# Half a 64-byte line between the weight tiles and the activation tiles of a two-block float32 transformer on one core

## The chip, the cores and the metric

One core of a Trainium2 chip runs the whole program in one launch. The metric is device time in microseconds (us), the median of several executions. Before the change it is 1710.91 us, the median of three runs between 1709.13 and 1711.71.

## The reference, cut to what matters

Two transformer blocks of different kinds, each two layers deep, work on x of 256 tokens by 1024 features in float32. Nearly all of the arithmetic is products of activations with weight matrices that come from HBM:

```python
for l in range(2):                                   # first block
    h = rms_norm(x, attn_norm[l]) @ w_in[l]          # then three kinds of attention
    x = x + mix @ w_o[l]
    gate, up = split(rms_norm(x, ffn_norm[l]) @ w_gate_up[l])
    x = x + (silu(gate) * up) @ w_down[l]            # 2816 hidden features
for l in range(2):                                   # second block
    h = rmsnorm(x, ...) @ w_in_2[l]                  # pool, convolution, dilated attention, gates
    x = x + rmsnorm(merged @ w_out_2[l], ...)
    x = x + rmsnorm(memory_cross_attention(...), ...)
    x = x + rmsnorm((silu(conv(h @ up_a)) * (h @ up_b)) @ w_down_2[l], ...)
```

## The kernel before, in words

**Layout.** Everything is feature-major: a tile `[128, k, 256]` holds 128 features of a slot k in its partitions and the 256 tokens along the free axis, 1024 bytes a slot. T is 256, PAIR is 512 and KD, the number of slots of x, is 8.

**Products.** Each float32 operand is split in a high part, rounded to the format fp32r, and a low part, the rest. A product is then three matmuls: low weights by high activations (L775, in `products`), high weights by low activations (L777), high by high (L778). `first_products` does the same for the first jobs after a norm (L732, L735, L741). There the stationary operand, read by a weight load (LDWEIGHTS), is a 128x128 piece of a weight tile, and the moving operand is a 256-column slot of an activation tile. Jobs with `feature=False` turn the roles round (L784, L786, L787): activations are loaded, weights move.

**Weights.** They are packed by the host in chunks of 1536 columns, 6144 bytes in each partition. SyncE issues the DMAs (L2540) into a ring of five tiles `raw`; ScalarE rounds a chunk into one of four `weights_hi` (L636, `split_hi`); VectorE writes raw minus high into one of four `weights_lo` (L647, `split_lo`), GpSimd for a few chunks (L660, `pool_lo`). A chunk's slots come free when TensorE is past them. Jobs are in a fixed order for each layer, written out by hand; each engine follows it with its own helpers.

**SBUF.** `place` puts tiles one behind the other, each rounded up to 8 words (32 bytes). The 13 weight tiles come first, then `x`, `y`, `squares`, then `minus_half`, and behind that `x_hi` and `x_lo`, the norm's small tiles, `row`, `quiet`, the gains, the constants (with the identity matrix `ident` for transposes) and the area `arena`, in which both blocks keep their mixing and feed-forward activations at different times:

```python
def place(name, cols, dt=F32, at=None):
    ...
    at = cursor[0]
    cursor[0] += -(-n // 8) * 8
...
X = place("x", (KD, T))
Y = place("y", (KD, T))
SQ = place("squares", (KD, T))
HALF = place("minus_half", 16)
XH = place("x_hi", (KD, T), F32R)
XL = place("x_lo", (KD, T), F32R)
```

`HALF` is filled with -0.5 once (L2626) and read as an exponent by six small GpSimd operations (L1401). `QUIET` is filled with zeros (L2625); `keep_busy` (L708) multiplies it with itself, one column broadcast to 128, in front of some waits of TensorE.

Of the kernel before, what the change touches and what calls it, by code (L numbers as in the profile page):

```python
# [298 lines left out]
def gain_places(block):  # L299
    at, n = {}, 0  # L300
    for name, c in gain_columns(block):
        at[name] = n
        n += 1 if c == -1 else abs(c)
    return at, n
# [103 lines left out]
def transformer(nc, known, stream_a, jobs_a, stream_b, jobs_b, const_at,  # L408
                x_in, mem_in, pos_in, w_a, w_b, gains_a, gains_b, consts, out):
    ctx = ExitStack()  # L410
    with ctx:
# [10 lines left out]
        def place(name, cols, dt=F32, at=None):  # L422

            cols = (cols,) if isinstance(cols, int) else cols
            n = math.prod(cols)
            if at is None:
                at = cursor[0]
                cursor[0] += -(-n // 8) * 8
            assert at + n <= end, (name, at + n, end)
            t = nc.alloc_sbuf_tensor_at(name, [P, *cols], dt, offset=base + 4 * at)  # L430
            return t
# [22 lines left out]
        X = place("x", (KD, T))  # L454
        Y = place("y", (KD, T))
        SQ = place("squares", (KD, T))
        HALF = place("minus_half", 16)
        XH = place("x_hi", (KD, T), F32R)
        XL = place("x_lo", (KD, T), F32R)
        PART = place("merge_part", PAIR)  # L460
# [7 lines left out]
        OROOT = place("dif_root", 16)  # L468
        OFACT = place("dif_factor", 16)
        T1 = place("t1", PAIR)  # L470
        T2 = place("t2", PAIR)
        ROW = place("row", 64)
        QUIET = place("quiet", 8)
        _, na = gain_places(0)
        _, nb = gain_places(1)
        GA = place("gains_a", (DEPTH, na))
# [228 lines left out]
        def keep_busy(ps, n):  # L705

            for _ in range(n):
                nc.tensor.matmul(ps[:, T:T + P], QUIET[:, 0:1].to_broadcast([P, P]), QUIET[:, 0:1].to_broadcast([P, P]), start=True, stop=True, skip_group_check=True)  # L708

# [689 lines left out]
        def pool_power(dst, src, half):  # L1399

            return nc.gpsimd.tensor_tensor(dst, src, half, ALU.pow)  # L1401

        def pool_factor(pl, pool, l, name):
# [3 lines left out]
            pool.wait_ge(*s.at(l, "qk_mean", QK_NAMES[b - 1]))  # L1407
            pool_power(HFACT[:, a:b, 0:4], HROOT[:, a:b, 0:4], HALF[:, 0:12].rearrange("p (a n) -> p a n", n=4)).then_inc(*s.mark("by_pool", name))

# [10 lines left out]
        def pool_dif_factor(pl, pool, l):  # L1420

            s = A
            pool.wait_ge(*s.at(l, "dif_root"))
            pool_power(OFACT[:, :], OROOT[:, :], HALF[:, :]).then_inc(*s.mark("by_pool", "dif"))

        def tensor_a(pe, l):
            A.layer = l
# [1166 lines left out]
        def pool_layer(pl, pool, l, order):  # L2594
            pl.s.layer, pl.s.writing = l, "pool"
            pl.pool_next, pl.pool_ahead = pl.pool_ahead, 0
            for kind, name in order:
                if kind == "first_chunks":
                    pool_lo(pl, pool, l, 1)
                if kind == "mem_squares" and l == 0:  # L2600
                    pool_mem_sum(pool)
                if kind == "adds" or kind == "norm":
                    pool_norm(pl, pool, l, name)
                elif kind == "roots" and name in ("uk", "uq"):
                    pool_factor(pl, pool, l, name)
                elif kind == "scale" and name[0] == "u":
                    pool_scale(pl, pool, l, name)
                elif kind == "dif_sum":
                    pool_dif_factor(pl, pool, l)
                elif kind == "job":  # L2610
                    pool_lo(pl, pool, l, pl.last_chunk(name) + 2)
                    if name == "down3":
                        pool_next_chunks(pl, pool, l)
# [10 lines left out]
        def _(dve):  # L2624
            nc.vector.memset(QUIET[:, :], 0.0)  # L2625
            nc.vector.memset(HALF[:, :], -0.5)  # L2626
            nc.vector.memset(eps_col, EPS).then_inc(*O.mark("eps"))
# [70 lines left out]
```

## Time and profile before

| | us |
|---|---|
| median of three runs | 1710.91 |
| the profiled execution, as timed | 1712.45 |
| its span, from the first to the last instruction | 1710.6 |
| TensorE matmul busy | 1672.5 |
| TensorE weight load busy | 1610.7 |
| VectorE busy | 1195.9 |
| ScalarE busy | 895.9 |
| GpSimd busy | 113.9 |

TensorE's mean granted clock is 0.996 of full speed. Matmuls are pipelined, so that the duration of one (some 280 ns) is longer than the time from the start of one to the start of the next (some 115 ns). The latter is what adds up to the span; it is had by dividing a stretch that has no break by the matmuls in it. Each stretch counts an instruction that crosses its edge, so a count can be two or three too high.

### The profile page before, as it was taken

How to read it: one execution, taken by the hardware profiler on the slowest of the kernel's cores; microseconds unless marked ns; L12 is line 12 of the kernel's file. 1: busy time of each engine (PE TensorE's matmuls, PEld its weight loads, DVE VectorE, ACT ScalarE, POOL GpSimd, SP SyncE). 2: the span in 40 equal slices, each digit the busy share in tenths (PEclk: the TensorE clock that was granted, in tenths of full speed). 3: DMA queues.
4: the chain of work that ended last, by engine and by line, in shares of the span. 5: the costliest groups of instructions: out<-in, count | busy, mean ns of one | idle time of the engine just before them, and what ended most of it. 6: DMA issues, size and time to landing. Idle time of an engine off the chain costs nothing.

```text
span 1710.6 us, 31850 instructions
## 1 busy us (share of the span) xinstructions
PE 1672.5 (98%) x13590; PEld 1610.7 (94%) x13590; DVE 1195.9 (70%) x1745; ACT 895.9 (52%) x1366; POOL 113.9 (7%) x72
## 2 busy tenths in 40 slices
PE   9989999999899999999999999999999999999997
PEld 9978999999789999989999989999899999899997
DVE  5887767557867675476758768973667768669863
ACT  5575544455765444544545765544534446656542
POOL 2020000020100000210000110001100001010000
PEclk9999999999999999999999999999999999999999
DMA  8313555554235555545345335555445445346550
GB/s 290 101 63 122 193 187 178 174 194 139 75 108 194 197 180 182 214 163 189 112 137 192 122 131 202 199 171 176 157 154 168 140 148 185 117 148 202 198 184 28
DMA packets 52830, 274.31 MB, mean 160 GB/s; under 512 B 6096, under 2 KB 6736, under 8 KB 52560
## 3 DMA queue, kind: packets, MB, share of 16 engines
q1 hardware_dynamic: 52544, 271.22, 46.6%
q8 instruction: 107, 1.75, 0.4%
q10 hardware_dynamic: 144, 1.05, 0.2%
q14 instruction: 35, 0.29, 0.0%
HBM read 271.19 MB, written 1.05 MB: 159 GB/s over the span
## 4 chain that ended last, share of the span: by engine, by line
PE 81%; DVE 13%; ACT 3%; issue 2%; DMA 1%; SPq 0%; ACTq 0%; DVEq 0%
PE bank L775 17%; PE bank L778 17%; PE bank L777 17%; PE scores L775 3%; PE scores L777 3%; PE scores L778 3%; DVE weights_lo L647 2%; PE heads L775 2%; PE heads L778 2%; PE heads L777 2%; DVE x_lo L900 1%; PE scores L1849 1%; ACT probs L1170 1%; PE heads L1877 1%; DVE x L2340 1%
## 5 line engine op out<-in xcount | busy, mean ns | idle before, releaser
L647 DVE TENSOR_TENSOR weights_lo<-raw,weights_hi 128x1536 fp32r<-128x1536 f32 (+2 forms) x344 | 584.2, 1715 | 244.3 <-ACT weights_hi L636 243.9
L636 ACT ACTIVATE weights_hi<-raw 128x1536 fp32r<-128x1536 f32 (+4 forms) x352 | 499.8, 1439 | 210.6 <-PE bank L778 87.2
L775 PE MATMUL bank<-x_hi,weights_lo 128*128 128x256 f32 (+1 forms) x1600 | 452.4, 283 | 0.8 <-DVE weights_lo L647 0.8
L778 PE MATMUL bank<-x_hi,weights_hi 128*128 128x256 f32 (+1 forms) x1600 | 446.5, 279 | 0.0
L777 PE MATMUL bank<-x_lo,weights_hi 128*128 128x256 f32 (+1 forms) x1600 | 446.1, 279 | 0.0
L775 PEld LDWEIGHTS bank<-x_hi,weights_lo 128*128 128x128 f32 (+1 forms) x1600 | 298.2, 186 | 6.1 <-issue 4.8
L777 PEld LDWEIGHTS bank<-x_lo,weights_hi 128*128 128x128 f32 (+1 forms) x1600 | 298.8, 187 | 2.0 <-issue 2.0
L778 PEld LDWEIGHTS bank<-x_hi,weights_hi 128*128 128x128 f32 (+1 forms) x1600 | 298.5, 187 | 0.0
L775 PE MATMUL bank<-hidden_hi,weights_lo 128*128 128x256 f32 x704 | 196.2, 279 | 0.0
L777 PE MATMUL bank<-hidden_lo,weights_hi 128*128 128x256 f32 x704 | 196.1, 279 | 0.0
L778 PE MATMUL bank<-hidden_hi,weights_hi 128*128 128x256 f32 x704 | 196.1, 279 | 0.0
L778 PEld LDWEIGHTS bank<-hidden_hi,weights_hi 128*128 128x128 f32 x704 | 133.0, 189 | 0.0
L777 PEld LDWEIGHTS bank<-hidden_lo,weights_hi 128*128 128x128 f32 x704 | 132.8, 189 | 0.0
L775 PEld LDWEIGHTS bank<-hidden_hi,weights_lo 128*128 128x128 f32 x704 | 132.2, 188 | 0.2 <-DVE hidden_lo L2194 0.2
L775 PE MATMUL scores<-x_hi,weights_lo 128*128 128x256 f32 x416 | 116.2, 279 | 0.9 <-DVE weights_lo L647 0.9
L778 PE MATMUL scores<-x_hi,weights_hi 128*128 128x256 f32 x416 | 116.3, 280 | 0.0
L777 PE MATMUL scores<-x_lo,weights_hi 128*128 128x256 f32 x416 | 116.3, 279 | 0.0
L834 POOL TENSOR_TENSOR squares<-squares 128x512 f32<-128x512 f32 x28 | 51.5, 1838 | 841.4 <-ACT squares L2123 648.3
L775 PEld LDWEIGHTS scores<-x_hi,weights_lo 128*128 128x128 f32 x416 | 78.0, 187 | 1.2 <-issue 1.2
L777 PEld LDWEIGHTS scores<-x_lo,weights_hi 128*128 128x128 f32 x416 | 78.1, 188 | 0.0
L778 PEld LDWEIGHTS scores<-x_hi,weights_hi 128*128 128x128 f32 x416 | 78.0, 187 | 0.0
L775 PE MATMUL heads<-x_hi,weights_lo 128*128 128x256 f32 x256 | 71.8, 280 | 0.4 <-DVE weights_lo L647 0.4
(410 smaller groups left out, 3395.2 us busy)
## 6 DMA issues: line engine op xcount, KB each, us to landing
raw<-in_w_b SPq DMA_DIRECT2D x194, 768.0 KB, 4.2
raw<-in_w_a SPq DMA_DIRECT2D x120, 768.0 KB, 4.3
raw<-in_w_a SPq DMA_DIRECT2D x16, 512.0 KB, 3.6
raw<-in_w_b SPq DMA_DIRECT2D x10, 512.0 KB, 4.0
raw<-in_w_b SPq DMA_DIRECT2D x2, 752.0 KB, 4.5
raw<-in_w_a SPq DMA_DIRECT2D x2, 736.0 KB, 8.6
raw<-in_w_b SPq DMA_DIRECT2D x2, 720.0 KB, 4.7
raw<-in_w_a SPq DMA_DIRECT2D x2, 672.0 KB, 7.3
```

The costliest lines, as they stand in the source:

```text
L636: nc.scalar.activation(whi[c % SPLIT][:, 0:n], raw[c % RAW][:, 0:n], ACT.Copy).then_inc(*s.mark("weights_hi", c))
L647: nc.vector.tensor_tensor(wlo[c % SPLIT][:, 0:n], raw[c % RAW][:, 0:n], whi[c % SPLIT][:, 0:n].bitcast(F32), ALU.subtract).then_inc(*s.mar ...
L775: ins = nc.tensor.matmul(dst, wl, xh, start=start, stop=False, skip_group_check=skip)
L777: nc.tensor.matmul(dst, wh, xl, start=False, stop=False, skip_group_check=skip)
L778: ins = nc.tensor.matmul(dst, wh, xh, start=False, stop=stop, skip_group_check=skip)
L834: nc.gpsimd.tensor_tensor(sq[:, 0:2, :], sq[:, 0:2, :], sq[:, 2 * n:2 * n + 2, :], ALU.add).then_inc(*s.mark("sq_pairs", (tag, n)))
L900: nc.vector.scalar_tensor_tensor(out=XL[:, k, :], in0=X[:, k, :], scalar=gains(k), in1=XH[:, k, :].bitcast(F32), op0=ALU.mult, op1=ALU.sub ...
L1170: ins = nc.scalar.activation(PA[c][:, m, :], score_bank[c][:, m * T:(m + 1) * T], ACT.Exp, scale=f[:, m:m + 1], bias=ROW[:, r + m:r + m + ...
L1849: ins = nc.tensor.matmul(dil_scores(h, m, g), QKB[r, f // 2, m * P:(m + 1) * P], QKB[r, 6 + f // 2, 0:dil_tiles(m) * P], start=True, stop= ...
L1877: ins = nc.tensor.matmul(out_bank[rows, m * P:(m + 1) * P], VB[:, kt, f * DHD:(f + 1) * DHD], PTB[:, g * kts + kt, :], start=(n == 0), sto ...
L2340: nc.vector.tensor_tensor(x, x, y, ALU.add).then_inc(*s.mark("x_new", (tag, last)))
```

## The change

`quiet` (8 words) takes the place of `minus_half` (16 words) ahead of `x_hi`, and `minus_half`, now 24 words of which the same 16 are read at most, takes the place of `quiet` behind `row`. No instruction is added, removed or moved in time; the first `memset` of `HALF` writes 24 columns where it wrote 16.

```diff
         SQ = place("squares", (KD, T))
-        HALF = place("minus_half", 16)
+        QUIET = place("quiet", 8)
         XH = place("x_hi", (KD, T), F32R)
         XL = place("x_lo", (KD, T), F32R)
         PART = place("merge_part", PAIR)
@@
         ROW = place("row", 64)
-        QUIET = place("quiet", 8)
+        HALF = place("minus_half", 24)
         _, na = gain_places(0)
@@
-            pool_power(OFACT[:, :], OROOT[:, :], HALF[:, :]).then_inc(*s.mark("by_pool", "dif"))
+            pool_power(OFACT[:, :], OROOT[:, :], HALF[:, 0:16]).then_inc(*s.mark("by_pool", "dif"))
```

In bytes from the first weight tile, whose ring and `x`, `y`, `squares` keep their places:

| tiles | place before, mod 128 | after, mod 128 |
|---|---|---|
| `raw`, `weights_hi`, `weights_lo`, `x`, `y`, `squares` | 0 | 0 |
| `x_hi`, `x_lo`, `merge_part` and the small tiles up to `row` | 64 | 32 |
| `const` (with `ident`) | 32 | 64 |
| `const_b` | 64 | 96 |
| `arena`: mix, hidden, memory and their parts | 64 | 96 |

## Rows read from the trace of the kernel before

**Rows 1.** The page: span, and busy time of each engine.

```profile
span 1710.6 us, 31850 instructions
PE 1672.5 (98%) x13590; PEld 1610.7 (94%) x13590; DVE 1195.9 (70%) x1745; ACT 895.9 (52%) x1366; POOL 113.9 (7%) x72
```

**Rows 2.** The page: the chain that ended last, by engine.

```profile
PE 81%; DVE 13%; ACT 3%; issue 2%; DMA 1%; SPq 0%; ACTq 0%; DVEq 0%
```

**Rows 3.** Stretches without a break: hidden (four rows), gate and up (last).

```profile
core 0: us, PE busy (x) PEld busy (x) DVE busy (x) ACT busy (x) POOL busy (x), PEclk, DMA share, GB/s
305.00:355.00 50.00, 50.00 (x443) 50.00 (x442) 24.50 (x19) 21.53 (x18) 0.29 (x1) 1.00 0.49 162
650.00:700.00 50.00, 50.00 (x427) 50.00 (x426) 24.51 (x19) 19.52 (x17) 0.00 (x0) 1.00 0.46 158
1140.00:1190.00 50.00, 49.97 (x441) 49.78 (x440) 24.89 (x20) 24.26 (x26) 0.90 (x1) 1.00 0.43 145
1640.00:1690.00 50.00, 50.00 (x426) 50.00 (x426) 22.30 (x17) 22.65 (x24) 3.33 (x3) 1.00 0.37 122
210.00:260.00 50.00, 50.00 (x426) 50.00 (x426) 36.74 (x43) 22.50 (x21) 0.00 (x0) 1.00 0.56 191
```

**Rows 4.** Groups by line, 302.6 to 363 us (first block, layer 0, down).

```profile
L778 PE MATMUL bank<-hidden_hi,weights_hi 128*128 128x256 f32 x176 | 48.6, 276 | 0.0
L778 PEld LDWEIGHTS bank<-hidden_hi,weights_hi 128*128 128x128 f32 x176 | 33.0, 188 | 0.0
```

**Rows 5.** The same groups, 646.3 to 709 us (layer 1, down).

```profile
L778 PE MATMUL bank<-hidden_hi,weights_hi 128*128 128x256 f32 x176 | 49.5, 281 | 0.0
L778 PEld LDWEIGHTS bank<-hidden_hi,weights_hi 128*128 128x128 f32 x176 | 33.8, 192 | 0.0
```

**Rows 6.** Stretches with the quick spacing: four of ten, and their sum.

```profile
302.60:363.20 60.60, 59.93 (x529) 1.00 0.53 184
484.40:505.70 21.30, 21.30 (x174) 1.00 0.33 103
760.40:808.80 48.40, 48.40 (x417) 1.00 0.51 171
1138.50:1198.40 59.90, 59.87 (x528) 1.00 0.49 171
...
sum 297.10, PE 296.41; mean PE 29.64
```

**Rows 7.** The whole span of one line each: L775, L784, L732.

```profile
0.00:1711.00 1711.00, 961.85 (x3416) 1.00 0.47 160
0.00:1711.00 1711.00, 136.19 (x444) 84.52 (x444) 1.00 0.47 160
0.00:1711.00 1711.00, 50.06 (x192) 35.99 (x192) 1.00 0.47 160
```

**Rows 8.** Groups by line and shape: moving `ident` (first), moving `v_b` (second).

```profile
L1105 PE MATMUL turned<-const,probs 128*128 128x128 f32 x128 | 18.0, 278 | 3.8 <-DVE probs L1147 2.6 <-DVE probs L1153 1.1
L1877 PE MATMUL heads<-probs_tb,v_b 128*64 128x128 f32 x144 | 19.1, 278 | 0.0
```

**Rows 9.** Waits: who waited for whom, us in total, times, longest.

```profile
DVE weights_lo L647 <- ACT weights_hi L636: 243.9, 137, 7.9
ACT weights_hi L636 <- PE bank L778: 87.2, 40, 3.1
PE bank L775 <- DVE weights_lo L647: 3.6, 3, 2.8
```

**Rows 10.** The moved small tiles: instructions that touch them.

```profile
L2626 DVE MEMSET minus_half<- x1: 72/72/72, 0.8 to 0.8; 128x16 f32 x1
L2625 DVE MEMSET quiet<- x1: 65/65/65, 0.8 to 0.8; 128x8 f32 x1
L1401 POOL TENSOR_TENSOR dif_factor<-dif_root,minus_half x2: 2901/2901/2901, 125.3 to 473.3; 128x16 f32<-128x16 f32 x2
```

**Rows 11.** Groups by line and shape: reads and writes of moved tiles on VectorE.

```profile
L900 DVE SCALAR_TENSOR_TENSOR x_lo<-x,gains_b,x_hi 128x256 fp32r<-128x256 f32 x48 | 19.5, 478 | 0.0
L2194 DVE TENSOR_TENSOR hidden_lo<-t,hidden_hi 128x256 fp32r<-128x256 f32 x44 | 16.6, 420 | 7.0 <-ACT hidden_hi L2156 7.0
L647 DVE TENSOR_TENSOR weights_lo<-raw,weights_hi 128x1536 fp32r<-128x1536 f32 x314 | 548.3, 1761 | 228.3 <-ACT weights_hi L636 227.9
```

## The prediction, made before the changed kernel was run

> **What bounds the kernel now.** I read the page's busy times first: TensorE is busy 98% of the span with matmuls and 94% with weight loads, VectorE 70%, ScalarE 52% [rows 1]. The chain that ended last lies on TensorE for 81%, and for 13% on VectorE [rows 2]. So the spacing of TensorE's own matmuls sets the end. Next I took stretches without a break, where all matmuls have one shape, 256 columns against a 128x128 weight load, and divided [rows 3]. Counts include what crosses an edge, so I take two off each. The down products of the first block's layer 0 come to 441 in 50 us, 113.4 ns each; those of layer 1 to 425, 117.6 ns. The same pair comes back in the second block: 439 (113.9) and 424 (117.9). Gate and up products: 424, 117.9. [...] The code, the tiles and the places in SBUF of layers 0 and 1 are the same, and other engines do much the same work (VectorE 24.5 against 24.5 us). So there are **two steady spacings**, about 113.4 and 117.8 ns, and the stream keeps the one it has fallen into. In the slow one a matmul takes 281 ns for 276, and the weight load at L778 192 for 188 [rows 4, 5]: the load is held up as well as the matmul. That looks like two streams that both read SBUF, the weight load and the moving operand, and get in each other's way depending on how they are phased.
>
> [...]
>
> [...]
>
> [...]
## The result: 1718.57 us against 1709.97, half a per cent slower

The changed kernel takes 1718.57 us, the median of five runs (1717.72 to 1719.94). The kernel before, in five runs, takes 1709.97 (1708.69 to 1711.71). The ratio is 1.0042 with a 95% interval of 1.0031 to 1.0054. Forecast was 1676 us with 0.27 on slower.

The page of the changed kernel, with the lines that answer to [rows 1, 2]:

```profile
span 1716.5 us, 31850 instructions
PE 1679.4 (98%) x13590; PEld 1618.1 (94%) x13590; DVE 1194.9 (70%) x1745; ACT 895.9 (52%) x1366; POOL 114.0 (7%) x72
...
PE 83%; DVE 11%; ACT 3%; issue 2%; DMA 1%; SPq 0%; ACTq 0%; DVEq 0%
```

The span grew by 5.9 us, TensorE's busy time by 6.9, its weight loads' by 7.4; VectorE, ScalarE and GpSimd did not change by more than 1 us. So most of the time is in TensorE's own spacing. The stretches of [rows 3], in the changed kernel; gate and up first here, then the four down stretches:

```profile
core 0: us, PE busy (x) PEld busy (x) DVE busy (x) ACT busy (x) POOL busy (x), PEclk, DMA share, GB/s
210.00:260.00 50.00, 50.00 (x430) 50.00 (x430) 37.16 (x43) 22.54 (x22) 0.00 (x0) 1.00 0.57 192
305.00:355.00 50.00, 50.00 (x425) 50.00 (x424) 24.50 (x19) 19.96 (x17) 0.00 (x0) 1.00 0.45 153
650.00:700.00 50.00, 50.00 (x425) 50.00 (x424) 24.50 (x19) 20.56 (x17) 0.00 (x0) 1.00 0.44 146
1140.00:1190.00 50.00, 50.00 (x425) 50.00 (x424) 23.42 (x21) 22.73 (x27) 0.00 (x0) 1.00 0.42 143
1640.00:1690.00 50.00, 50.00 (x425) 50.00 (x425) 24.05 (x22) 22.72 (x27) 2.10 (x2) 1.00 0.35 122
```

The quick spacing of before is gone, and there are two new ones that go with the tile. Down products, with the moving tile at 96 mod 128, count 425 in all four stretches, 423 after the two for the edges: 118.2 ns (from the start times in ns, 118.33). Gate and up, which move x at 32, count 430: 116.8 (116.67). Neither is 113.4, neither is 117.8. One long kind of stretch keeps 117.8 though x moves there at 32 as well, the products of the second block's feed-forward in both layers (a count of 427, as in the kernel before):

```profile
1060.00:1110.00 50.00, 50.00 (x427) 50.00 (x426) 46.40 (x64) 28.60 (x33) 0.00 (x0) 1.00 0.60 200
```

So the place 32 has two spacings too, 116.7 and 117.8. Products that load x and move weights lost 4.9 ns each where they had been quick (first block, from 57 us; the first row is the kernel before, the second in its own fence the changed one):

```profile
57.00:68.00 11.00, 11.00 (x100) 11.00 (x99) 10.84 (x16) 7.05 (x22) 0.00 (x0) 1.00 0.54 174
```

```profile
57.50:68.50 11.00, 11.00 (x95) 11.00 (x95) 10.84 (x16) 6.83 (x21) 0.00 (x0) 1.00 0.55 175
```

In this stretch and its fellow in layer 1 they went at 113.4 before and at 118.3 after; other stretches of the kind were at 117.8 before. Counted over the whole trace from the start times, 256-column products that do not follow a wait (intervals of 100 to 160 ns):

| products | count | before, mean ns | after, mean ns | us |
|---|---|---|---|---|
| move x | 7049 | 117.44 | 117.03 | -2.9 |
| move hidden | 2107 | 115.57 | 118.33 | +5.8 |
| load x, move weights | 830 | 115.54 | 118.27 | +2.3 |
| move mix | 454 | 116.11 | 118.33 | +1.0 |
| move memory and its heads | 377 | 115.7 | 118.4 | +1.0 |

That is +7.2 us; pool tiles and loads of 96 columns add about 1. The span of the one traced pair took 5.9 of the 8. The medians are 8.6 us apart, and the traced execution of before, at 1712.45, was slower than all five runs of that kernel in the comparison, so how much of the 8 reaches the end is known only within some 2 us.

The prediction's points 2 to 4 in the changed kernel: VectorE's groups by line and shape, then the waits (who waited for whom, us in total, times, longest), then the instruction that writes the moved small tile:

```profile
L900 DVE SCALAR_TENSOR_TENSOR x_lo<-x,gains_b,x_hi 128x256 fp32r<-128x256 f32 x48 | 19.5, 482 | 0.0
L2194 DVE TENSOR_TENSOR hidden_lo<-t,hidden_hi 128x256 fp32r<-128x256 f32 x44 | 16.7, 421 | 7.0 <-ACT hidden_hi L2156 7.0
```

```profile
DVE weights_lo L647 <- ACT weights_hi L636: 246.3, 137, 7.9
ACT weights_hi L636 <- PE bank L778: 90.2, 41, 3.2
```

```profile
L2626 DVE MEMSET minus_half<- x1: 78/78/78, 0.8 to 0.8; 128x24 f32 x1
```

VectorE reads and writes tiles half a line off at 482 and 421 ns, against 478 and 420 in [rows 11]. The waits are those of [rows 9], 2.4 and 3.0 us longer, as they should be behind a slower TensorE.

### The profile page after: what moved, and what is told of

Read it like the earlier page. It is cut to its first block, busy times and chain, and to the rows that moved or that the text cites. A ratio compares the mean times of both kernels' runs of the same rounds, so it can differ in the third digit from the quotient of the medians.

```text
span 1716.5 us, 31850 instructions
## 1 busy us (share of the span) xinstructions
PE 1679.4 (98%) x13590; PEld 1618.1 (94%) x13590; DVE 1194.9 (70%) x1745; ACT 895.9 (52%) x1366; POOL 114.0 (7%) x72
## 4 chain that ended last, share of the span: by engine, by line
PE 83%; DVE 11%; ACT 3%; issue 2%; DMA 1%; SPq 0%; ACTq 0%; DVEq 0%
PE bank L775 17%; PE bank L778 17%; PE bank L777 17%; PE scores L775 3%; PE scores L778 3%; PE scores L777 3%; DVE weights_lo L647 2%; PE heads L775 2%; PE heads L778 2%; PE heads L777 2%; PE bank L784 1%; PE bank L787 1%; PE bank L786 1%; DVE x_lo L900 1%; ACT probs L1170 1%
## 5 line engine op out<-in xcount | busy, mean ns | idle before, releaser
L647 DVE TENSOR_TENSOR weights_lo<-raw,weights_hi 128x1536 fp32r<-128x1536 f32 (+2 forms) x344 | 584.5, 1716 | 246.7 <-ACT weights_hi L636 246.3
L775 PE MATMUL bank<-x_hi,weights_lo 128*128 128x256 f32 (+1 forms) x1600 | 453.5, 283 | 0.4 <-DVE weights_lo L647 0.4
L775 PEld LDWEIGHTS bank<-x_hi,weights_lo 128*128 128x128 f32 (+1 forms) x1600 | 299.0, 187 | 5.7 <-issue 4.8
L775 PE MATMUL bank<-hidden_hi,weights_lo 128*128 128x256 f32 x704 | 197.8, 281 | 0.0
L775 PEld LDWEIGHTS bank<-hidden_hi,weights_lo 128*128 128x128 f32 x704 | 132.6, 188 | 0.0
L775 PE MATMUL scores<-x_hi,weights_lo 128*128 128x256 f32 x416 | 116.5, 280 | 0.9 <-DVE weights_lo L647 0.9
L775 PEld LDWEIGHTS scores<-x_hi,weights_lo 128*128 128x128 f32 x416 | 78.2, 188 | 1.2 <-issue 1.2
L775 PE MATMUL heads<-x_hi,weights_lo 128*128 128x256 f32 x256 | 71.9, 281 | 0.4 <-DVE weights_lo L647 0.4
```

Source lines behind the costliest of these rows:

```text
L647: nc.vector.tensor_tensor(wlo[c % SPLIT][:, 0:n], raw[c % RAW][:, 0:n], whi[c % SPLIT][:, 0:n].bitcast(F32), ALU.subtract).then_inc(*s.mar ...
L775: ins = nc.tensor.matmul(dst, wl, xh, start=start, stop=False, skip_group_check=skip)
```

## Experiments

The theory after the result: the spacing of the matmul and weight-load stream goes with the distance, mod 128 bytes, between the tile that moves and the tile that is loaded. At 64 there are two possible spacings, at 32 and 96 others. The rival: the time lost has to do with a restart's phase alone, or with tiles that straddle 64-byte lines, whatever the distance. Two terms: "place" is bytes mod 128 from the first weight tile, "distance" is the place of the moving tile minus that of the loaded one. Mod 128 hides a difference that the end of the section on tables takes up: by the sizes in the code, x_hi and x_lo stand at 64 and the areas at 192 mod 256 before, at 32 and 224 after, with all weight tiles at 0.

### Each part of the change alone

x at 32, areas at 64:

```diff
-        HALF = place("minus_half", 16)
+        QUIET = place("quiet", 8)
 ...
-        QUIET = place("quiet", 8)
+        HALF = place("minus_half", 16)
```

> Only x_hi, x_lo and the small tiles go half a line off (32 bytes mod 128); the areas with mix, hidden and memory stay at 64. Theory 1, the spacing follows from the place of the activation tile: products that move x go at 116.7 ns a matmul as in the changed kernel (140 fewer of a cycle each than 117.8), products that load x and move weights at 118.3, and the down products keep the two spacings of before (113.4 or 117.8). Sum: x moved saves some 8 us in the slow stretches and gives 2 back in the quick ones, x loaded costs 3: 1706 to 1709 us, against 1710. Rival, the spacing is set by the phase at a restart and not by the place: the down products change too, or the x products stay at 117.8; time within 2 us of before.

Measured: 1706.71 us (nine runs) against 1710.56, ratio 0.9976, interval 0.9966 to 0.9987. This part alone is a gain.

Areas at 96, x at 64:

```diff
-        QUIET = place("quiet", 8)
+        QUIET = place("quiet", 16)
```

> Only the areas go to 96 mod 128; x_hi and x_lo stay at 64. Theory 1: down products 118.3 ns in both layers of both blocks, no quick spacing left in them nor in mix and memory products; x products as before, with both spacings. Cost: 1,056 down products lose 5.0 ns, 1,056 lose 0.55, mix and memory some 3 us: 8 to 10 us over before, 1718 to 1720. Rival: the areas alone change nothing that can be measured and the loss comes of both offsets together: 1709 to 1712.

Measured: 1719.77 us (five runs) against 1710.56, ratio 1.0054, interval 1.0042 to 1.0067. This part alone is a little more than the whole loss. The windows of both, gate and up then layer 0's down, x part alone:

```profile
210.00:260.00 50.00, 50.00 (x431) 50.00 (x430) 35.26 (x40) 23.54 (x22) 0.00 (x0) 1.00 0.57 198
305.00:355.00 50.00, 50.00 (x443) 50.00 (x443) 23.08 (x19) 19.50 (x16) 2.39 (x1) 1.00 0.54 188
```

and the areas alone:

```profile
210.00:260.00 50.00, 50.00 (x427) 50.00 (x426) 35.09 (x39) 23.19 (x22) 0.00 (x0) 1.00 0.57 192
305.00:355.00 50.00, 50.00 (x424) 50.00 (x424) 24.01 (x19) 19.45 (x16) 0.42 (x1) 1.00 0.47 163
```

Each family follows its own tile: 431 and 424 for the moved ones, 443 and 427 for those left at 64. In the traced execution with x at 32 the down products had the quick spacing in all four stretches (113.4 ns), not in two of four as in the trace of before, though their own place had not changed. That is 2107 matmuls by 2.2 ns, 4.6 us. What goes with the place of x is less: x moved saves 3.5 us (116.95 for 117.44), and x loaded gives 2.3 back. The expectation had the down products unchanged, so that its total was right by luck in part.

That moving x put the down products into the quick spacing is not shown. Which of them are quick differs between executions of one layout. The kernels with tables (below) run the kernel before and then a table. Their traces have the down stretches quick, quick, quick, slow; quick, slow, quick, slow; and slow, quick, quick, quick, the last one in these rows:

```profile
305.00:355.00 50.00, 50.00 (x427) 50.00 (x427) 24.51 (x19) 20.35 (x17) 0.00 (x0) 1.00 0.44 148
650.00:700.00 50.00, 50.00 (x443) 50.00 (x442) 27.96 (x26) 22.18 (x19) 0.00 (x0) 1.00 0.43 147
1140.00:1190.00 50.00, 49.96 (x440) 49.77 (x440) 24.43 (x23) 24.30 (x28) 0.00 (x0) 1.00 0.42 144
1640.00:1690.00 50.00, 50.00 (x441) 50.00 (x440) 24.60 (x19) 23.21 (x25) 3.34 (x3) 1.00 0.35 122
```

The layout with every tile shifted, distances as before, has all four quick in its trace as well, at an unchanged time. Whether the quick spacing became more frequent with x at 32 would take many traces of each.

### The two places swapped

```diff
-        HALF = place("minus_half", 16)
+        HALF = place("minus_half", 24)
 ...
-        QUIET = place("quiet", 8)
+        QUIET = place("quiet", 24)
```

> x_hi and x_lo at 96 mod 128 and the areas at 32: the two places of the changed kernel swapped. Theory 1 (the spacing follows from the distance mod 128 between the moving tile and the weights, by the table: 116.7 ns at 32, 118.3 to 120 at 96): down products 116.7 ns, x products 118 to 120. Some 8,000 products that move x lose 0.5 to 2.2 ns against 117.8, and 600 of their quick ones 5 to 6; down, mix and memory gain 1.1 on the slow half and lose 3.3 on the quick: 1717 to 1732 us. Rival (x and the areas differ for another reason, such as how far high and low tile are apart): x stays at 116.7 and down at 118.3, 1716 to 1720 us.

Measured: 1733.53 us (four runs) against 1709.07, ratio 1.0142, interval 1.0125 to 1.0159. Gate and up, then down:

```profile
210.00:260.00 50.00, 50.00 (x419) 50.00 (x418) 35.67 (x42) 22.79 (x21) 0.00 (x0) 1.00 0.57 191
305.00:355.00 50.00, 50.00 (x431) 50.00 (x430) 25.59 (x21) 20.91 (x17) 0.00 (x0) 1.00 0.42 137
```

Down has 431 now, the count that gate and up had at 32 (116.67 ns). x at 96 has 419, 119.96 ns. So at 32 the place decides, not what the tile holds. At 96 mod 128 there are two values, 118.33 with hidden in the changed kernel and 119.96 with x here; mod 256 these are two places, 224 and 96. The time came out just above the range of the expectation, because x took the upper of them throughout.

### Everything on the weights' grid

```diff
-        HALF = place("minus_half", 16)
+        HALF = place("minus_half", 32)
```

> x_hi, x_lo and the areas at 0 mod 128, the place of the weights. By the table's streams at distance 0 (118.6 to 120.0 ns): no 113.4 anywhere, 118.5 to 120 in every product, 10 to 25 us over before, 1720 to 1735. If only whole or half lines of 64 bytes counted, 0 would be as 64: 113.4 and 117.8, 1708 to 1713 us.

Measured: 1733.46 us in one run. 64 bytes off the grid and on it are not the same:

```profile
210.00:260.00 50.00, 50.00 (x424) 50.00 (x423) 36.31 (x41) 22.04 (x21) 0.00 (x0) 1.00 0.57 191
305.00:355.00 50.00, 50.00 (x419) 50.00 (x418) 24.50 (x19) 20.54 (x17) 0.00 (x0) 1.00 0.42 138
```

Down 119.97 ns, x moved 118.86. If places a whole number of 64-byte pieces apart were alike, this would be the kernel before; the line of 64 that the change speaks of is not the unit. Nor are hidden and x alike here, both at 0 mod 128: mod 256 they stand at 0 and 128.

### Distance, or how a tile lies on the lines

```diff
-        base = -(-nc.sbuf_base // 32) * 32
+        base = -(-nc.sbuf_base // 32) * 32 + 32
```

> The layout of before, every tile with it the weights moved up by 32 bytes: distances between tiles are those of before, but each tile now starts half way into a 64-byte line. Theory A, the distance between loaded and moving tile counts: spacings 113.4 and 117.8 and 1708 to 1712 us, as before. Theory B, what counts is how a slot lies on the lines: no 113.4 left, spacings of 116 to 119 as in the changed kernel, 1712 to 1725 us.

Measured: 1710.18 us (12 runs) against 1710.56, ratio 0.9996, interval 0.9984 to 1.0008.

```profile
210.00:260.00 50.00, 50.00 (x427) 50.00 (x426) 36.77 (x42) 22.91 (x21) 0.00 (x0) 1.00 0.57 191
305.00:355.00 50.00, 50.00 (x444) 50.00 (x443) 24.50 (x19) 21.88 (x18) 0.00 (x0) 1.00 0.47 158
```

The two layouts differ by half a 64-byte piece in where every tile starts, so that in one of them every slot touches a 17th, and neither the time nor the two spacings (113.4, 117.8) changed. The rival of a 17th line falls, and with it any cost of half-line tiles as such. What was changed by the edit in question is the distance. (In this trace all four down stretches are quick, 444, 444, 441 and 442, against two of four in the trace of before.)

### Tables on TensorE alone

`spacing_table` runs behind the last output's DMA, with all other engines at rest. A stream is 42 or 63 matmuls in the kernel's order (low weights by high x, high by low, high by high), from slices of `x_hi`, `x_lo` and two weight tiles that begin where wanted; some products of `quiet` stand ahead of each:

```diff
+        def spacing_table(pe):
+            pe.wait_ge(loaded["out_rest"], 16)
 ...
+            def stream(m, w, cols=T, rows=P, ahead=2, turns=3, roles=False):
+                keep_busy(ps, ahead)
 ...
+                        a, b = m + k * T, w + k * P
+                        for lw, mv in ((wlo[0], xh), (whi[0], xl), (whi[0], xh)):
```

> The kernel before, and behind its end 40 streams of 63 matmuls on TensorE alone, with the other engines at rest: moving operand at 0, 16, 32 to 112 bytes mod 128 twice, weights at 0, 32, 64, 96, narrow loads of 32, 64 and 96 columns, roles turned round, 192 columns. It adds some 300 us. [...] If the other engines' traffic makes the slow spacing, all streams with whole lines go at 113.4.

Spacing in ns from the start times, past the first 24 matmuls, weights at place 0, from two starts:

| moving tile at | 0 | 16 | 32 | 48 | 64 | 80 | 96 | 112 |
|---|---|---|---|---|---|---|---|---|
| 2 ahead | 118.8 | 118.8 | 118.8 | 119.2 | 113.3 | 118.3 | 120.0 | 113.3 |
| 5 ahead | 120.0 | 116.7 | 117.4 | 119.3 | 117.8 | 118.3 | 120.0 | 113.3 |

With the weights at 32, 64 and 96 the pattern goes with them: distance 32 gives 116.7 three times, 64 gives 117.8 three times. From 1715 us to the end of this trace VectorE, ScalarE and GpSimd are busy for 0.00 us and the DMA share is 0.00, so no other engine and no DMA is needed for either spacing, and at distance 64 the one place showed both, by the start alone. The narrow loads ran from one start each. With loads of only 32 columns and the moving tile at 64, 96, 0, 32 the spacings are 120.0, 117.5, 115.5 and 113.3, with 64 columns all four are 116.7, and with 96 they are 117.8, 117.8, 120.0 and 116.7: how long the load is changes the spacing, though at 108 ns for 32 columns, 134 for 64, 162 for 96 and 188 for 128 it is shorter than the matmul, some 276 to 283. That with a load of 32 columns every place goes at one spacing near 113 was an estimate of mine, and wrong. With 192 moving columns all four are at 111.6, so there the place costs nothing (loads 192 ns, matmuls 274); what sets the pace then was not shown.

The finer table, at each 4 bytes from three starts:

> Behind the kernel before, 96 streams of 42 matmuls, the moving operand at each multiple of 4 bytes from 0 to 124 mod 128 from the weights, each from three starts (2, 3 or 5 small products ahead), and 24 with the roles turned round at multiples of 16. It adds some 700 us. Theory (distance and start choose among a few fixed spacings): every stream settles at one of 113.3, 116.7, 117.8, 118.3 to 120 ns; at 112 all three at 113.3, at 64 113.3 or 117.8, at 32 mostly 116.7, at 0 and 96 118 to 120. Rival (the first table's differences are chance of the start): each place shows any spacing.

The third and the 39th matmul of a stream, so 36 intervals, distance 112, last start:

```profile
2245.10 0.28 PE L2537 MATMUL bank<-x_hi,weights_hi 128*128 128x256 f32 x1
...
2249.18 0.28 PE L2537 MATMUL bank<-x_hi,weights_hi 128*128 128x256 f32 x1
...
2171.43 0.28 PE L2537 MATMUL bank<-x_hi,weights_hi 128*128 128x256 f32 x1
...
2175.67 0.28 PE L2537 MATMUL bank<-x_hi,weights_hi 128*128 128x256 f32 x1
...
2220.44 0.28 PE L2537 MATMUL bank<-x_hi,weights_hi 128*128 128x256 f32 x1
...
2224.76 0.28 PE L2537 MATMUL bank<-x_hi,weights_hi 128*128 128x256 f32 x1
```

4.08 us by 36 is 113.3 ns at distance 112; the second pair, at 64, gives 4.24, 117.8; the third, at 96, 4.32, 120.0. Of 32 distances, with the weights at 0, one stands out: 113.35 at 112 from all three starts. All others lie between 116.6 and 124.4, past the first 24 matmuls (the very first stream begins at a granted clock of 0.50, 1710 to 1716 us). At 64 all three came at 117.8, at 32 118.6, 117.4 and 117.4. The theory of a few fixed spacings is too narrow, there are more of them, up to 124.4 at 4 bytes; the rival that place is chance is out, as the starts with 3 and 5 small products ahead agree within 0.1 ns at all 32, and that with 2 ahead within 0.3 at 20 of them.

The third table asks if the difference is all:

> Behind the kernel before, 88 streams of 42 matmuls, each from two starts: moving tile 112 and 64 bytes from the weights with the weights themselves at 0 to 112; the same tile for high and low part of the weights, of x, or of both; the weight load always at one address; roles turned round with x loaded 16 bytes past the weights that move (moving minus loaded is 112 again), at eight places. Theory D, only the difference mod 128 counts: all at 113.3 for 112, 113.3 or 117.8 for 64, the roles turned at 113.3 as well. Theory P, the place of the tiles counts too: 113.3 at 112 only with weights at 0 (or at multiples of 32), other spacings of 116 to 122 elsewhere, and turned roles at 118 to 120 as the last table showed for x at 16.

Distance 112 (112 up, or 16 down, from the weights), weights at 0 to 112, two starts (values within 0.4 of each other):

| weights at | 0 | 16 | 32 | 48 | 64 | 80 | 96 | 112 |
|---|---|---|---|---|---|---|---|---|
| ns | 113.3 | 120.0 | 113.4 | 120.0 | 113.3 | 118.3 | 117.2 | 118.4 |
| ns at distance 64 | 117.8 | 118.3 | 117.8 | 118.3 | 117.8 | 118.3 | 117.8 | 118.3 |
| weights moving, x loaded 16 further | 120.0 | 113.3 | 120.0 | 117.2 | 118.4 | 117.2 | 118.4 | 117.2 |

So the difference mod 128 alone is not the rule (Theory D): weights at 0 and at 16, or at 32 and at 96, differ. One tile for high and low part of the weights, of x or of both, and a load that always reads one address, changed nothing: 113.35 at 112, 117.8 at 64, 119.7 or 120.2 at 96 in all.

What separates 32 from 96 is in the edits. `x_hi` starts at 64 mod 256, and a stream begins 0 to 124 bytes behind that, so the moving tile stands 112 above the weights for weights at 0 to 64, and 16 below them, 240 mod 256, for 80 to 112. Counted mod 256, all 16 values at distance 112 fall in order, whichever tile is the loaded one: at 112, 113.3 when the loaded tile's place is a multiple of 32 and 120.0 when it is 16 beyond one; at 240, some 117.2 and 118.4. (At distance 64 it is 117.8 and 118.3.) For the same reason the columns 0 to 48 of the first table are 128 to 176 mod 256, and its 32 (118.8, 117.4) is not the 32 of the changed kernel. With the loaded tile at a multiple of 32, tables and kernels then agree:

| moving minus loaded, mod 256 | tables, ns | kernels, ns |
|---|---|---|
| 0 | 120.0 | all on the grid, hidden 119.97 |
| 32 | 116.7 | changed, x 116.67 (and 117.8); swapped, hidden 116.67 |
| 64 | 113.3 or 117.8 | before, x 113.3 or 117.8 |
| 96 | 119.7 to 120.2 | swapped, x 119.96 |
| 112 | 113.3 | the layout below, x and hidden 113.3 |
| 128 | 118.6 to 118.8, or 120.0 | all on the grid, x 118.6 or 120.0 |
| 192 | 113.3 or 117.7 (weights moving) | before, hidden 113.3 or 117.8, and x loaded |
| 224 | 118.4 | changed, hidden 118.33, and x loaded 118.3 |

This reading was made from traces at hand, and no run was built to test it; the layout below holds one case that it did not draw on.

### A layout at 112

Every fp32r activation tile starts at 112 mod 128. The kernel's own `place` puts tiles at multiples of 32 bytes, so each is a view 16 bytes into a tile at 96:

```diff
+        def first(name, dt, at):
+            if dt == F32R and not name.startswith("weights"):
+                return at + (28 - at) % 32
+            return at // 8 * 8 if dt == I32 else -(-at // 8) * 8
 ...
+            t = nc.alloc_sbuf_tensor_at(name, [P, at % 8 + n], dt, offset=base + 4 * (at - at % 8))
+            return t[:, at % 8:].rearrange("p (a n) -> p a n", a=cols[0])
 ...
-        POS = place("positions", T, I32, a1.at - T)
+        POS = place("positions", T, I32, end - T - 8)
```

> Every fp32r activation tile starts at 112 mod 128, by placing it 16 bytes into a tile that is allocated at 96; weights as before. The table's two streams there both went at 113.34 ns, from either start. If that holds beside the other engines' work: all products that move activations at 113.4, some 8,000 slow ones gain 4.4 ns, nine tenths of it at the end, 30 to 38 us saved; products with roles turned round lose or gain up to 3 us: 1672 to 1683 us. Rival (the quick spacing is only a matter of the start, as at 64): a mixture of 113.4 and 117 to 119, 1690 to 1712 us. Positions are kept at the end of SBUF, out of the way of the moved tiles.

Measured: 1685.66 us (four runs) against 1709.07, ratio 0.9867, interval 0.9852 to 0.9882. That is faster than the kernel before by 1.3%, and its median lies 33 us under that of the changed one. Its page, and two windows:

```profile
span 1683.5 us, 31850 instructions
PE 1645.4 (98%) x13590; PEld 1582.5 (94%) x13590; DVE 1194.5 (71%) x1745; ACT 896.1 (53%) x1366; POOL 115.0 (7%) x72
...
PE 77%; DVE 15%; ACT 4%; issue 2%; DMA 0%; POOL 0%; SPq 0%; ACTq 0%; DVEq 0%; POOLq 0%
```

```profile
210.00:260.00 50.00, 50.00 (x443) 50.00 (x442) 36.66 (x41) 23.57 (x22) 0.00 (x0) 1.00 0.59 204
305.00:355.00 50.00, 50.00 (x443) 50.00 (x443) 21.25 (x16) 20.78 (x21) 4.39 (x2) 1.00 0.57 204
57.00:68.00 11.00, 11.00 (x94) 11.00 (x93) 10.86 (x16) 6.79 (x21) 0.00 (x0) 1.00 0.57 181
```

Gate and up have 443 in 50 us where they had 426: the quick spacing, in x products too (mean 113.80 over 7042, for 117.44, 25.6 us) and hidden (113.42, 4.5 us). Products that load x are worse, 94 in 11 us, 119.9 for 115.5, 3.6 us lost, as the tables have it for weights moving at 0. Together 26.5 and some 1 us for mix: 27, and the span is 27.1 shorter than that of the trace of before; the medians are 23.4 apart. The upper end of the expectation, 1672 to 1683, was 3 us too low: it counted 8,000 matmuls that went at 117.8 before at a full 4.4 ns, while the mean of x products stayed at 113.8, and took the loss at the turned roles at 3 at most. VectorE has room at this speed as well: it makes TensorE wait for `weights_lo` at the same line for 3.8 us, against 3.6 in [rows 9].

```profile
PE bank L782 <- DVE weights_lo L654: 3.8, 5, 2.8
```

(The lines of this kernel stand 7 lower.)

One pair of tiles tests the reading mod 256. `mem_hi` and `mem_lo` stand at 112, `mem_o_hi` and `mem_o_lo` at 240, and both are at 112 mod 128. The products of the first (first row) go at the quick spacing, 113.3; those of the second (second row), over 85 intervals, at 117.1, where the tables have 117.2 to 117.4 for 240:

```profile
946.00:951.00 5.00, 5.00 (x47) 5.00 (x46) 4.25 (x5) 3.62 (x5) 3.10 (x2) 1.00 0.48 157
979.00:988.00 9.00, 9.00 (x78) 9.00 (x78) 2.45 (x2) 6.78 (x13) 2.03 (x2) 1.00 0.25 89
```

## Why the prediction was wrong

**What bounds the kernel: right.** TensorE's own spacing sets the time. There were two spacings at the same places, 113.4 and 117.8; the table reproduces both with the other engines at rest. That the load is held up with the matmul in a slow spacing is not general: in the changed kernel's down products the matmul takes 281 ns as at the slow spacing of [rows 5], and the load 188 as at the quick one.

```profile
L778 PEld LDWEIGHTS bank<-hidden_hi,weights_hi 128*128 128x128 f32 x142 | 26.8, 188 | 0.0
```

**Part 1, the step that failed.** "I take the lower end as likeliest": that half a line would take the two streams out of each other's way, all 8,700 slow matmuls then at 113.4. What the runs showed: half a line has spacings of its own. At 32 it is 116.7, a gain of 1.1 ns where the spacing was 117.8 and a loss of 3.3 where it was 113.4, or 117.8 still; where the areas went (96 mod 128) it is 118.3, a loss on both. The term of -38 us came out at +8. The argument went from "a phase is worth 4.4 ns" to "this shift is the right phase", and no row had shown any product with such a shift. Why half a line should do it was my supposition: no run shows a unit of 64 bytes, and the run with all tiles on the grid speaks against it. The count of slow matmuls was an estimate as well, and it held: of the 12,156 products of weights in the trace of before 11,760 move 256 columns, and the 11,518 of these that are followed by the next within 100 to 160 ns have a mean spacing of 116.76 ns, so that 113.4 in all of them would have been worth 39 us. (Nine tenths of 9,550 are 8,600, not 8,700; that is 0.4 us.) The forecast also treated 32 and 96 as one case, since both are half a line off; they lie on either side of before.

**The nearest row misled.** `ident` and `v_b` at 278 ns [rows 8] are plain float32 products of 128 columns. The table has four places at one spacing, 111.6 ns, as soon as the moving operand is 192 columns wide, so a row of 128 could not bound a loss at 256. It also compares durations, and these tell the quick spacing from the slow by 5 ns only (276 and 281 in [rows 4, 5]).

**Part 2, the share that reaches the end: not contradicted.** Nine tenths was taken. By the traced pairs 5.9 of 8 us came through in the changed kernel and all of some 27 in the layout at 112; by the medians 8.6 of 8 and 23.4 of 27. **Parts 3 and 4: right.** VectorE's splits are 4 ns and 1 ns longer, GpSimd's power takes 2.9 us as before, and the `memset` 78 ns for an estimated 80.

**The rivals.** The sign and size of "the slow spacing wins everywhere", +11 us, come nearest to the measured +8.6, and its first test held: the down products of layers 0 lost the quick spacing. Its mechanism is only half right, so that the nearness of its size is luck in part. Hidden, mix and memory do lose the quick spacing at every restart, but to a third one, and x, the largest group, gained on the whole. "Partly" had seen that tiles at 32 and at 96 could differ, but only as gains. "No effect" is out: the parts alone give ratios of 0.9976 and 1.0054, with intervals that exclude 1 on either side. The 17th line is out by the shifted base, and by the counts of 425 and 430 where it wanted fewer than 415. Loads do not leave matmuls alone: with places held and the load's width changed from 128 to 32 columns in the table, the spacing at 64 went from 113.3 or 117.8 to 120.0, and at 32 from 118.8 or 117.4 to 113.3. That this is a conflict at SBUF, and not elsewhere in TensorE's input, was not shown.

**What stays open.** The cause behind the spacings: why each distance mod 256 has the one that it has, and why the loaded tile's place mod 32 counts. Which event at a start chooses where there are two. The period of 256 rests on a reading after the fact and on one pair of tiles; no run varied it by itself.

## What to carry to other kernels

Where TensorE streams weight loads and matmuls of 256 fp32r columns back to back, the relative place of the two tiles in SBUF moved the spacing between 113 and 120 ns here, some 6%, without a change to any instruction. It was not to be reasoned out from line sizes: a table of streams behind the real kernel costs one run and gives it for each offset, and should cover 256 bytes at least, with both tiles' places written down. And a spacing that comes in two values at one place flips from execution to execution of one kernel, here worth 2.3 us for each run of 528 matmuls: a single trace before and after can't tell such a flip from the work of an edit.

## What the runs showed that I had not expected

Of 32 places at 4-byte steps, with the weights at 0, exactly one had the quick spacing from every start, and it lies between the multiples of 32 at which `place` puts tiles. A weight load of 32 columns does not free the matmul: 120.0 ns at a place where 128 columns had 113.3 or 117.8. Two tiles at the same place mod 128 in one kernel, `mem_hi` and `mem_o_hi` in the layout at 112, went at 113.3 and 117.1 ns. And the kernel before, traced four times, alone and ahead of the tables, had two, three, two and three of its four down stretches quick, not the same ones.
